# Gated-recurrence heads: seven levels in the first half of a head, the next head's gates, logarithms and scans and this head's output in the second

## The chip, the core and the metric

The kernel runs on one core of a Trainium2 chip. The core has five engines with a queue each: TensorE (PE, with PEld for its weight loads), VectorE (DVE), ScalarE (ACT), GpSimd (POOL) and SyncE (SP), which issues the DMAs. An engine takes its instructions in the order in which they are written, and waits for another one by a semaphore that this other one raises. The metric is the device time of one execution in microseconds, the median of several runs.

## What is computed

The program is a whole two-layer block: a first mixer, a second mixer and an expert layer, on 512 grid tokens and 256 context tokens of width 1024. The change lies in one stage of the second mixer, the gated-recurrence heads. There are eight heads of 128 channels. What a head computes, from the reference:

```python
def hgrn2_forget(f_raw, lb):
    f = lb + (1 - lb) * jax.nn.sigmoid(f_raw.astype(jnp.float32))
    return jnp.log(f), 1 - f
...
    def step(s, inp):
        qc, kc, vc, gc = inp
        gcum = jnp.cumsum(gc, axis=2)
        decay = jnp.exp(jnp.where(causal[:, :, None],
                                  gcum[:, :, :, None, :] - gcum[:, :, None, :, :], -jnp.inf))
        att = jnp.einsum('bhtd,bhtsd,bhsd->bhts', qc, decay, kc)
        glast = gcum[:, :, -1:, :]
        o = (jnp.einsum('bhts,bhsv->bhtv', att, vc)
             + jnp.einsum('bhtd,bhdv->bhtv', qc * jnp.exp(gcum), s))
        s = (jnp.exp(glast[:, :, 0, :, None]) * s
             + jnp.einsum('bhsd,bhsv->bhdv', kc * jnp.exp(glast - gcum), vc))
        return s, o
...
    o = rms_norm(o_f + _flip(o_b), lw['hg_norm_w']).astype(u.dtype)
    o = o * jax.nn.silu(og.reshape(b, t, HG_HEADS, HG_DV))
```

It runs forward and backward over the tokens; both start from a state made by the context tokens. Queries are `silu(q)`. The five inputs of a head (forward forget gate, backward forget gate, query, value, output gate) are products of the normed tokens with five slices of `w_in_2`.

## The kernel before

All of it is in `gated_heads`. Tokens lie in columns, channels in partitions; the 768 tokens are six chunks of 128, two of the context and four of the grid.

**The projection.** A head has five tiles of weights, in the order FF and FB (the two forget gates), Q, V, G (the output gate). SyncE loads each (512 KB) into one of two buffers. ScalarE rounds it (`high`), VectorE subtracts the rounded part from it (`low`), and TensorE multiplies in three products of rounded and remaining parts (`product3`, L243 to L245). The results are cut into eight lots of a head: FF, FB and V have two of 384 columns, Q and G one of 512. A lot is eight units, each of three matmuls; a head thus has 64 units. TensorE does them between the steps of the head before: `fill(count)` takes the next `count` units. Lots alternate between two banks of PSUM, and ScalarE copies a finished lot out (`evict`), which frees its bank.

**A head.** The forget gates go through a sigmoid (`forget`), an affine map (`affine`), a logarithm (`logs`) and a scan that restarts at each chunk (`scan`, into `hg_cum`), forward and backward. `decays` makes the exponentials for the states, `weighted` multiplies them with keys (`hg_kd`) and queries (`hg_qe`). The attention within a chunk of 128 is cut into the diagonal and seven levels of blocks of 1, 2, 4 up to 64 tokens. For a level GpSimd takes two differences of the scans (`diff`, into one of two buffers `hg_dec`), ScalarE takes their exponential in place, VectorE multiplies it with keys and queries (`mixed`, into one of two buffers `hg_mix`), TensorE makes the products (`products`), and VectorE puts them where the level's mask is set (`kept`). `products(0)` is the diagonal, from queries and the sum of keys.

Beside that, TensorE turns the values and, once per direction, the weighted keys into rows; ScalarE copies these out (`hg_vt`, `hg_ktok`); TensorE makes the state updates from them, and VectorE folds the updates into states (`states`). The output is one sum of matmuls from `att` and the states, with its squares (`squares`), their sum by a matmul with ones, the root (`rstd`), and the products `pre` and `tail` with the output gate (`opened`). The query's sigmoid is in `forget` too.

**What sets the order.** A head is a loop over `at` = 1 to 14 on TensorE, ScalarE and VectorE, each with its own list of what stands at which step. A level stands at every second step, 1, 3, up to 13. On ScalarE, step 10 switches the table of functions to the sigmoid and back, and step 12 to the logarithm and back; level 7's exponential is at step 13. The output of a head comes after its step 14, its squares, root and tail at steps 1 to 3 of the next head. GpSimd has only the differences in its queue; it starts a head's when its two scans are done.

## Time and profile before

| | |
|---|---|
| median of 3 runs | 4962.45 us (4962.09 to 4962.82) |
| the profiled execution | 4965.7 us, its span 4963.9 us |
| span of this stage, first weight load to last product | 1449 to 2013 us |
| TensorE busy, whole span | 4008.9 us (81%) |
| VectorE busy | 2604.1 us (52%) |
| ScalarE busy | 1629.9 us (33%) |
| GpSimd busy | 957.4 us (19%) |

Times in the views count from the start of the span. "Busy" of TensorE is counted from modelled ends of pipelined matmuls, so rows of a matmul overlap the next one's start; how long one holds the engine is read from start to start. In a timeline row, `[3.13 <-DVE hg_mix L2685]` says that the engine was idle for 3.13 us before it, and that VectorE's instruction of line 2685 ended that. PEclk is the clock granted to TensorE, 1.00 being 2.4 GHz and 0.50 being 1.2 GHz. About a ninth of the program's time lies in this stage; stages before and after it are the same in both kernels.

### The profile page before, as it was taken

What the parts mean: (1) busy time and instruction counts of PE and PEld (TensorE: products, weight loads), DVE (VectorE), ACT (ScalarE), POOL (GpSimd) and SP (SyncE); (2) the same over time, 40 slices, a digit from 0 to 9 for tenths busy, and PEclk for the clock granted to TensorE, in tenths of its full rate; (3) what the DMA queues carried; (4) which work ended last, traced back from release to release, by engine and by line L of the source; (5) the groups of instructions that cost most, each with busy time, mean ns of one, the idle gap of its engine ahead of it and who ended that gap; (6) DMA issues with size and microseconds to landing.
All of it is one profiled execution on the core that took longest, in us unless ns stands there. A gap on an engine that the chain in (4) does not pass through costs nothing. (4 is left out here: it accounts for less than half of the span.)

```text
span 4963.9 us, 53777 instructions
## 1 busy us (share of the span) xinstructions
PE 4008.9 (81%) x20047; PEld 3308.9 (67%) x20047; DVE 2604.1 (52%) x4384; ACT 1629.9 (33%) x2422; POOL 957.4 (19%) x540
## 2 busy tenths in 40 slices
PE   6445599795948887588887798399897999999996
PEld 5344589662937776577776454287776878888884
DVE  0263678401046666367777201399995545555555
ACT  0332334211034444245455200332563222222222
POOL 0122300120003333011111110043223422222221
PEclk9677899997568998799999899699998999999998
DMA  3100010122411110111110221133456533333332
GB/s 134 45 1 26 22 36 30 34 73 102 157 34 39 43 39 22 40 35 47 43 43 30 115 85 47 51 113 100 136 189 234 196 132 123 127 127 106 122 117 69
DMA packets 134940, 404.74 MB, mean 82 GB/s; under 512 B 16352, under 2 KB 54992, under 8 KB 125008
## 3 DMA queue, kind: packets, MB, share of 16 engines
q1 hardware_dynamic: 134736, 402.01, 23.9%
q8 instruction: 130, 2.13, 0.2%
q14 instruction: 74, 0.61, 0.0%
HBM read 349.51 MB, written 52.45 MB: 81 GB/s over the span
## 5 line engine op out<-in xcount | busy, mean ns | idle before, releaser
L2237 POOL TENSOR_TENSOR ex_vl<-ex_v,ex_vh 128x1024 fp32r<-128x1024 f32 x80 | 192.1, 2401 | 685.6 <-ACT ex_vh L2225 685.6
L243 PE MATMUL ps<-ex_xh,ex_ul 128*128 128x512 f32 x640 | 250.1, 391 | 9.9 <-DVE ex_ul L2244 9.9
L243 PE MATMUL ps<-hT_high,ma_wl 128*128 128x384 f32 (+1 forms) x576 | 233.7, 406 | 25.2 <-DVE ma_wl L3156 25.2
L244 PE MATMUL ps<-ex_xl,ex_uh 128*128 128x512 f32 x640 | 249.7, 390 | 0.0
L245 PE MATMUL ps<-ex_xh,ex_uh 128*128 128x512 f32 x640 | 249.7, 390 | 0.0
L243 PE MATMUL ps<-ex_vh,ex_al 128*128 128x512 f32 x640 | 249.0, 389 | 0.0
L244 PE MATMUL ps<-ex_vl,ex_ah 128*128 128x512 f32 x640 | 249.0, 389 | 0.0
L245 PE MATMUL ps<-ex_vh,ex_ah 128*128 128x512 f32 x640 | 249.0, 389 | 0.0
L2221 ACT ACTIVATE ex_ab<-ps 128x512 f32<-128x512 f32 x80 | 47.8, 598 | 611.2 <-PE ps L245 611.2
L2263 DVE TENSOR_TENSOR ex_acc<-ex_acc,ps 128x512 f32<-128x512 f32 x160 | 109.7, 687 | 248.0 <-PE ps L245 248.0
L1465 DVE TENSOR_TENSOR mg_sg<-mg_sg,ps 128x512 f32<-128x512 f32 x32 | 22.0, 687 | 404.8 <-PE ps L1435 404.2
L2258 DVE TENSOR_TENSOR ex_al<-ex_af,ex_ah 128x512 fp32r<-128x512 f32 x80 | 198.1, 2477 | 61.1 <-ACT ex_ah L2227 61.1
L2400 POOL TENSOR_TENSOR hg_dec<-hg_cum 128x512 f32<-128x512 f32 x56 | 82.3, 1470 | 728.6 <-DVE hg_cum L2664 577.5
L150 PE MATMUL ps<-cond,mod_w 128*128 128x2 f32 x768 | 164.1, 352 | 69.7 <-DMA mod_w<-in_w_ada_cols 42.8
L2852 POOL TENSOR_TENSOR ma_ce<-ma_ce,ma_c 128x512 f32<-128x512 f32 x64 | 94.1, 1470 | 639.6 <-ACT ma_ce L3055 639.6
L243 PE MATMUL ps<-hT_high,hg_wl 128*128 128x384 f32 (+1 forms) x512 | 194.0, 379 | 22.6 <-DVE hg_wl L2640 22.6
L150 PEld LDWEIGHTS ps<-cond,mod_w 128*128 128x128 f32 x768 | 164.0, 333 | 70.5 <-issue 70.5
L245 PE MATMUL ps<-hT_high,ma_wh 128*128 128x384 f32 (+1 forms) x576 | 207.1, 360 | 0.0
L244 PE MATMUL ps<-hT_low,ma_wh 128*128 128x384 f32 (+1 forms) x576 | 206.9, 359 | 0.0
L244 PE MATMUL ps<-hT_low,hg_wh 128*128 128x384 f32 (+1 forms) x512 | 186.7, 365 | 0.0
L245 PE MATMUL ps<-hT_high,hg_wh 128*128 128x384 f32 (+1 forms) x512 | 185.8, 363 | 0.0
L1969 DVE TENSOR_SCALAR sg_two<-iota,chosenT 128x128 f32<-128x128 f32 x512 | 183.6, 418 | 0.0
(510 smaller groups left out, 11064.3 us busy)
## 6 DMA issues: line engine op xcount, KB each, us to landing
ex_u<-in_peer_u SPq DMA_DIRECT2D x80, 512.0 KB, 4.3
ex_v<-in_peer_v SPq DMA_DIRECT2D x80, 512.0 KB, 4.3
gates_by_expert<-sg_gbuf SPq DMA_DIRECT2D x8, 4096.0 KB, 15.1
ma_w<-in_w_in_ma SPq DMA_DIRECT2D x48, 512.0 KB, 3.6
ev_v<-in_peer_v SPq DMA_DIRECT2D x48, 512.0 KB, 3.5
hg_w<-in_w_in_hg SPq DMA_DIRECT2D x40, 512.0 KB, 3.5
ex_g<-gates_by_expert SPq DMA_DIRECT2D x20, 1024.0 KB, 4.8
mg_wg<-in_w_merge SPq DMA_DIRECT2D x16, 1024.0 KB, 5.0
```

The costliest lines, as they stand in the source:

```text
L150: mm = pe.matmul(ps[:, n % 2, 2 * a:2 * a + 2], wt[:, a, k, :], conds[:, k, :], start=(k == 0), stop=(k == KD - 1))
L243: pe.matmul(out, a[1], b[0], start=start, stop=False)
L244: pe.matmul(out, a[0], b[1], start=False, stop=False)
L245: return pe.matmul(out, a[0], b[0], start=False, stop=stop)
L1465: link(dve.tensor_tensor(sg[:, n % 2, a, :], sg[:, n % 2, a, :], ps[:, b + 2 + a, :], ALU.mult))
L1969: ins = dve.tensor_scalar(two[:, t0 + a, :], iota, chosenT[:, 1, t:t + 1], chosenT[:, 2, t:t + 1], ALU.is_equal, ALU.mult)
L2221: act.activation(ab[:, j % 2, :], ps[:, j % 2, :], ACT.Gelu).then_inc(h_read, 1)
L2237: pool.tensor_tensor(vl[:, j], v[:, j % 2], vh[:, j].bitcast(F32), ALU.subtract).then_inc(vl_ready, 1)
L2258: dve.tensor_tensor(al[:, j], af[:, j % 2], ah[:, j].bitcast(F32), ALU.subtract).then_inc(al_ready, 1)
L2263: dve.tensor_tensor(acc[:, n // 2, n % 2, :], acc[:, n // 2, n % 2, :], ps[:, 2 + n % VB, :], ALU.add).then_inc(v_read, 1)
L2400: pool.tensor_tensor(ke, crossed(cums[:, h % 2], size, False, True), crossed(cums[:, h % 2], size, False, False), ALU.subtract)
L2852: pool.tensor_tensor(ce[:, i % 2], ce[:, i % 2], cT[:, P * c:P * c + P].unsqueeze(1).to_broadcast([P, J, P]), ALU.mult).then_inc(ce_scaled, 1)
```

## The change

All seven levels move to steps 1 to 7 of a head, one per step. The second half has the next head's sigmoids (8, 9), affine maps, logarithms and scans (9 to 11), and this head's output (10), squares (11), sum (12), root and tail (13, 14). The query's sigmoid becomes a step of its own (`asked`), and both `decays` and `weighted(h + 1, 0)` of the next head are done by its start. The turning of the values goes behind level 1's products. A table `FILL` gives the units of the projection for each step, 64 in all, as before; evictions are placed where these units end. One of the four table loads per head falls away: behind the sigmoids the logarithm's table comes at once. The instructions on TensorE are the same ones.

```diff
-        LOW_AT = (1, 3, 6, 10, 13)
+        FILL = (4, 5, 5, 5, 5, 5, 5, 5, 5, 4, 5, 4, 4, 3)
...
                     products(0)
                     for at in range(1, 2 * LV + 1):
...
+                        if at <= LV:
+                            products(at)
+                        if at == 1:
+                            pe.wait_ge(evicted, lot_of(h, V, 1) + 1)
                             for c in range(NC):
-                                mm = pe.transpose(turn(c), kds[:, dr, P * c:P * c + P], k.ident[:])
+                                mm = pe.transpose(turn(c), v[:, P * c:P * c + P], k.ident[:])
                                 if c in (3, NC - 1):
-                                    mm.then_inc(kt_done, 1)
-                        if at % 2 == 1:
-                            products((at + 1) // 2)
-                        fill(5 if at <= 8 else 4 if at <= 10 else 2 if at % 2 else 1)
-                        if at in (2, LV + 2):
-                            pe.wait_ge(kt_copied, 2 * u + 2)
-                            if u > 0:
-                                pe.wait_ge(S_ready, u)
-                            for c in ORDER[dr][:-1]:
-                                mm = pe.matmul(U(c), ktok[:, c, :], vt[:, c, :], start=True, stop=True)
-                            mm.then_inc(u_done, 1)
-                    fill(2)
-                    pe.wait_ge(att_kept, (h + 1) * (LV + 1))
-                    pe.wait_ge(S_ready, 2 * h + 2)
-                    for c in range(NXC):
-                        o = ps[:, 5, P * c:P * c + P]
-                        pe.matmul(o, vt[:, C0 + c, :], att[:, c, :], start=True, stop=False)
-                        for dr in range(2):
-                            slot = ORDER[dr][C0:].index(C0 + c)
-                            mm = pe.matmul(o, S[:, dr, slot, :], qe[:, p, dr, P * c:P * c + P], start=False, stop=(dr == 1))
-                    mm.then_inc(o_done, 1)
-                    fill(8)
-                    pe.wait_ge(sq_ready, h + 1)
-                    pe.wait_ge(pre_ready, h + 1)
-                    pe.matmul(ps[:, 5, :], k.ones[:], scr[:], start=True, stop=True).then_inc(ss_done, 1)
+                                    mm.then_inc(vt_done, 1)
+                        if at == 2:
+                            key_rows(0)
+                        if at == 3:
+                            updates(0)
+                        if at == 5:
+                            key_rows(1)
+                        if at == 6:
+                            updates(1)
+                        if at == 10:
+                            pe.wait_ge(att_kept, (h + 1) * (LV + 1))
+                            pe.wait_ge(S_ready, 2 * h + 2)
+                            for c in range(NXC):
+                                o = ps[:, 5, P * c:P * c + P]
+                                pe.matmul(o, vt[:, C0 + c, :], att[:, c, :], start=True, stop=False)
+                                for dr in range(2):
+                                    slot = ORDER[dr][C0:].index(C0 + c)
+                                    mm = pe.matmul(o, S[:, dr, slot, :], qe[:, p, dr, P * c:P * c + P], start=False, stop=(dr == 1))
+                            mm.then_inc(o_done, 1)
+                        if at == 12:
+                            pe.wait_ge(sq_ready, h + 1)
+                            pe.wait_ge(pre_ready, h + 1)
+                            pe.matmul(ps[:, 5, :], k.ones[:], scr[:], start=True, stop=True).then_inc(ss_done, 1)
+                        fill(FILL[at - 1])
...
+                decays(0, 1)
                 for h in range(H):
                     m, n, last = 8 * (h + 1), 5 * (h + 1), h + 1 == H
                     for at in range(1, 2 * LV + 1):
-                        dr = 0 if at <= LV else 1
-                        u = 2 * h + dr
-                        if at % 2 == 1:
-                            i = level_of(h, (at + 1) // 2)
+                        if at <= LV:
+                            i = level_of(h, at)
                             act.wait_ge(diff_ready, i)
                             act.activation(dec[:, (i - 1) % DEC], dec[:, (i - 1) % DEC], ACT.Exp).then_inc(dec_ready, 1)
                         if at == 1:
                             if h > 0:
-                                squares(h - 1)
+                                act.wait_ge(pre_ready, h)
+                            evict(lot_of(h, G))
                             for c0, c1, b in ((0, 4, 2), (4, 6, 3)):
                                 act.wait_ge(vt_done, 2 * h + b - 1)
                                 act.copy(vt[:, c0:c1, :], ps[:, b, 0:P * (c1 - c0)].rearrange("p (c t) -> p c t", c=c1 - c0)).then_inc(vt_copied, 1)
-                        if at in (2, LV + 2):
+                            high(n + FB)
+                        if at == 2 and not last:
+                            evict(m)
+                        if at in (2, 5):
+                            u = 2 * h + (0 if at == 2 else 1)
                             if u > 0:
                                 act.wait_ge(u_done, u)
                             for c0, c1, b in ((0, 4, 2), (4, 6, 3)):
                                 act.wait_ge(kt_done, 2 * u + b - 1)
                                 act.copy(ktok[:, c0:c1, :], ps[:, b, 0:P * (c1 - c0)].rearrange("p (c t) -> p c t", c=c1 - c0)).then_inc(kt_copied, 1)
-                        if at == 2:
-                            if h > 0:
-                                act.wait_ge(pre_ready, h)
-                            evict(lot_of(h, G))
-                            high(n + FB)
-                            if h > 0:
-                                rstd(h - 1)
-                        if not last:
-                            if at == 4:
-                                evict(m)
-                            if at == 5:
-                                evict(m + 1)
-                                high(n + Q)
-                            if at == 7:
-                                evict(m + 2)
-                            if at == 8:
-                                evict(m + 3)
-                                high(n + V)
-                            if at == 10:
-                                evict(m + 4)
-                                high(n + G)
-                        if at == 5:
-                            decays(h, 1)
-                        if at == 10:
+                        if at == 4 and not last:
+                            evict(m + 1)
+                            high(n + Q)
+                        if at == 5 and not last:
+                            evict(m + 2)
+                        if at == 7 and not last:
+                            evict(m + 3)
+                            high(n + V)
+                        if at == 8:
                             act.preload_act_table_set("sigmoid_and_others")
                             if not last:
                                 forget(h + 1)
+                        if at == 9:
+                            if not last:
+                                evict(m + 4)
+                                asked(h + 1)
+                                high(n + G)
                             act.wait_ge(evicted, lot_of(h, G) + 1)
                             opened(h)
-                            act.preload_act_table_set("natural_log_exp_and_others")
-                        if not last and at == 12:
-                            logs(h + 1)
-                    if not last:
-                        evict(m + 5)
-                        decays(h + 1, 0)
-                        evict(m + 6)
-                        high(n + 5 + FF)
-                squares(H - 1)
-                rstd(H - 1)
+                        if at == 10:
+                            if last:
+                                act.preload_act_table_set("natural_log_exp_and_others")
+                            else:
+                                evict(m + 5)
+                                logs(h + 1)
+                        if at == 11:
+                            squares(h)
+                        if at == 12 and not last:
+                            decays(h + 1, 0)
+                            decays(h + 1, 1)
+                            evict(m + 6)
+                        if at == 13:
+                            rstd(h)
+                        if at == 14 and not last:
+                            high(n + 5 + FF)
 
             @block.vector
             def _(dve):
...
+                    n, last = 5 * (h + 1), h + 1 == H
                     for at in range(1, 2 * LV + 1):
-                        if at % 2 == 1:
-                            mixed(h, (at + 1) // 2)
-                        if at in LOW_AT:
-                            low(5 * h + 5 + LOW_AT.index(at))
-                        if at == 1 and h > 0:
-                            pre(h - 1)
-                        if at % 2 == 1:
-                            kept(h, (at - 1) // 2)
-                        if at == 3 and h > 0:
-                            tail(h - 1)
+                        if at <= LV:
+                            mixed(h, at)
+                        if at == 2:
+                            low(n + FB)
+                        if at <= LV + 1:
+                            kept(h, at - 1)
+                        if at == 3:
+                            weighted(h, 1)
                         if at == 4:
                             states(h, 0)
-                        if at == 6:
-                            weighted(h, 1)
-                        if at == 11:
+                        if at == 5:
+                            low(n + Q)
+                        if at == 8:
+                            low(n + V)
                             states(h, 1)
-                        if at == 12 and h + 1 < H:
+                        if at == 9 and not last:
                             affine(h + 1, 0)
                             affine(h + 1, 1)
-                            query(h + 1)
+                        if at == 10:
+                            if not last:
+                                query(h + 1)
+                            opened(h)
+                            low(n + G)
+                        if at == 11 and not last:
+                            scan(h + 1, 0)
+                            scan(h + 1, 1)
                         if at == 12:
-                            opened(h)
-                    if h + 1 < H:
-                        scan(h + 1, 0)
-                    kept(h, LV)
-                    if h + 1 < H:
-                        scan(h + 1, 1)
-                pre(H - 1)
-                tail(H - 1)
+                            pre(h)
+                        if at == 13 and not last:
+                            weighted(h + 1, 0)
+                        if at == 14:
+                            tail(h)
+                            low(n + 5 + FF)
```

What moved, as the instructions stand in the engines' queues in a middle head. Line numbers of the changed kernel differ from those of the kernel before by a few. First ScalarE in the first half; `hg_dec` is a level's exponential, `hg_f<-ps` an eviction, the cast a rounding, `hg_ktok` the turned keys. Before:

```order
L2580 ACTIVATE hg_dec<-hg_dec 128x1024
L2510 COPY hg_f<-ps 128x384
L2580 ACTIVATE hg_dec<-hg_dec 128x1024
L2510 COPY hg_f<-ps 128x384
L2504 CAST hg_wh<-hg_w 128x1024
L2538 ACTIVATE hg_ebl<-hg_cum 128x6
L2540 ACTIVATE hg_qe<-hg_cum 128x512
L2542 ACTIVATE hg_kd<-hg_kd 128x768
L2580 ACTIVATE hg_dec<-hg_dec 128x1024
```

And changed, from level 2 to level 7:

```order
L2592 ACTIVATE hg_dec<-hg_dec 128x1024
L2520 COPY hg_f<-ps 128x384
L2609 COPY hg_ktok<-ps 128x512
L2609 COPY hg_ktok<-ps 128x256
L2592 ACTIVATE hg_dec<-hg_dec 128x1024 x2
L2520 COPY hg_f<-ps 128x384
L2514 CAST hg_wh<-hg_w 128x1024
L2592 ACTIVATE hg_dec<-hg_dec 128x1024
L2609 COPY hg_ktok<-ps 128x512
L2609 COPY hg_ktok<-ps 128x256
L2520 COPY hg_f<-ps 128x384
L2592 ACTIVATE hg_dec<-hg_dec 128x1024 x2
```

The exponentials of three levels (3, 5 and 6) now have an eviction of a lot ahead of them in the same half, with the copies of the keys or a rounding between. The second place is ScalarE from the sigmoids on. Before, `hg_f<-hg_f` of L2516 being the sigmoids and of L2531 the logarithms:

```order
L2617 ACT_TABLE_LOAD
L2516 ACTIVATE hg_f<-hg_f 128x768 x2
L2520 ACTIVATE hg_sg<-hg_q 128x512
L2525 ACTIVATE hg_sg<-hg_gate 128x512
L2622 ACT_TABLE_LOAD
L2580 ACTIVATE hg_dec<-hg_dec 128x1024
L2528 ACT_TABLE_LOAD
L2531 ACTIVATE hg_f<-hg_f 128x768 x2
L2532 ACT_TABLE_LOAD
L2580 ACTIVATE hg_dec<-hg_dec 128x1024
L2510 COPY hg_v<-ps 128x384
```

And changed, L2526 being the sigmoids, L2543 the logarithms and L2560 this head's squares:

```order
L2526 ACTIVATE hg_f<-hg_f 128x768 x2
L2520 COPY hg_q<-ps 128x512
L2532 ACTIVATE hg_sg<-hg_q 128x512
L2514 CAST hg_wh<-hg_w 128x1024
L2537 ACTIVATE hg_sg<-hg_gate 128x512
L2520 COPY hg_v<-ps 128x384
L2540 ACT_TABLE_LOAD
L2543 ACTIVATE hg_f<-hg_f 128x768 x2
L2544 ACT_TABLE_LOAD
L2560 ACTIVATE hg_scr<-ps 128x512
```

The exponentials of levels 6 and 7 have gone from between the table loads, and the first V lot's eviction now stands ahead of the logarithms.

## Rows read from the trace of the kernel before

**Rows 1.** Stretches of one head: window, length, busy us (count) per engine, PEclk, DMA.

```profile
1692.65:1759.30 66.65, 56.02 (x330) 52.30 (x329) 41.99 (x57) 33.05 (x47) 20.76 (x15) 0.92 0.13 40
1759.30:1827.46 68.16, 56.72 (x323) 53.11 (x322) 41.81 (x57) 32.22 (x46) 20.76 (x14) 0.90 0.13 39
```

**Rows 2.** Waits in 1692.65:1759.30: engine, line waited for: total, times, longest.

```profile
DVE hg_mix L2684 <- ACT hg_dec L2580: 20.5, 5, 8.2
```

**Rows 3.** TensorE in order of time: start, length, instruction, count [idle before].

```profile
1692.08 0.38 PE L2485 MATMUL ps<-hg_att,hg_vt 128*128 128x128 f32 x2
...
1694.67 0.47 PE L243 MATMUL ps<-hT_high,hg_wl 128*128 128x512 f32 x1
...
1701.83 1.10 PE L2493 MATMUL ps<-hg_scr,ones 128*128 128x512 f32 x2 [1.31 <-DVE oT L2717]
1702.76 0.82 PE L2437 MATMUL ps<-ident,hg_v 128*128 128x128 f32 x6
1703.41 1.06 PE L2453 MATMUL ps<-hg_q,hg_sg 128*128 128x128 f32 x8
...
1711.20 1.28 PE L2478 MATMUL ps<-hg_vt,hg_ktok 128*128 128x128 f32 x10
1712.31 1.06 PE L2453 MATMUL ps<-hg_mix 128*128 128x128 f32 x8
1713.12 0.42 PE L243 MATMUL ps<-hT_high,hg_wl 128*128 128x384 f32 x1
...
1718.43 1.05 PE L2453 MATMUL ps<-hg_mix 128*128 128x128 f32 x8
...
1742.21 1.75 PE L2453 MATMUL ps<-hg_mix 128*128 128x128 f32 x8 [3.13 <-DVE hg_mix L2685]
...
1752.68 2.04 PE L2453 MATMUL ps<-hg_mix 128*128 128x128 f32 x8 [6.18 <-DVE hg_mix L2685]
```

**Rows 4.** ScalarE in order of time, first half of the same head.

```profile
1705.12 0.86 ACT L2592 COPY hg_ktok<-ps 128x512 f32<-128x512 f32 x2 [0.86 <-PE ps L2467]
...
1716.55 0.48 ACT L2510 COPY hg_f<-ps 128x384 f32<-128x384 f32 x1 [4.75 <-PE ps L245]
1716.92 1.05 ACT L2504 CAST hg_wh<-hg_w 128x1024 fp32r<-128x1024 f32 x1
```

**Rows 5.** The page's DMA issues: tiles, count, KB each, us to landing.

```profile
hg_w<-in_w_in_hg SPq DMA_DIRECT2D x40, 512.0 KB, 3.5
```

**Rows 6.** ScalarE, second half: a logarithm, a table load, an exponential of a level.

```profile
1681.35 0.84 ACT L2531 ACTIVATE hg_f<-hg_f 128x768 f32<-128x768 f32 x1 [0.94 <-DVE hg_f L2647]
1682.21 1.28 ACT L2532 ACT_TABLE_LOAD   x1
1683.51 1.06 ACT L2580 ACTIVATE hg_dec<-hg_dec 128x1024 f32<-128x1024 f32 x1
```

**Rows 7.** VectorE: a scan, the keys' product twice, a mix.

```profile
1690.82 1.75 DVE L2664 TENSOR_TENSOR_SCAN hg_cum<-hg_restart,hg_f 128x768 f32<-128x768 f32 x1
...
1693.48 1.85 DVE L2674 TENSOR_TENSOR hg_kd<-hg_kd,hg_k 128x768 f32<-128x768 f32 x1
...
1719.76 0.94 DVE L2674 TENSOR_TENSOR hg_kd<-hg_kd,hg_k 128x768 f32<-128x768 f32 x1
...
1740.77 0.69 DVE L2684 TENSOR_TENSOR hg_mix<-hg_dec,hg_k 128x512 f32<-128x512 f32 x1 [8.18 <-ACT hg_dec L2580]
```

**Rows 8.** A stretch, TensorE alone: window, length, busy, PEclk, DMA.

```profile
1744.00:1746.00 2.00, 2.00 (x8) 0.51 0.00 0
```

**Rows 9.** TensorE, the next head's sum of squares.

```profile
1768.47 1.10 PE L2493 MATMUL ps<-hg_scr,ones 128*128 128x512 f32 x2 [2.11 <-DVE oT L2717]
```

**Rows 10.** TensorE, level 1 of the first head and the squares ahead of the last.

```profile
1503.27 2.08 PE L2453 MATMUL ps<-hg_mix 128*128 128x128 f32 x8 [0.15 <-DVE hg_mix L2685]
...
1968.85 1.10 PE L2493 MATMUL ps<-hg_scr,ones 128*128 128x512 f32 x2 [1.07 <-DVE oT L2717]
```

**Rows 11.** VectorE, the stage's last product.

```profile
2012.70 0.69 DVE L2723 TENSOR_TENSOR oT<-oT,hg_scr 128x512 f32<-128x512 f32 x1 [2.66 <-ACT hg_scr L2553]
```

36 lines of the change are left out of this document (22 added, 14 removed).

## The prediction

> **What bounds the kernel now.** I read the stretches by head first, then the waits inside one head, then TensorE's order of time, and last ScalarE and VectorE around the two long waits. The stage repeats itself once per head: one head takes 66.65 us from its first GpSimd subtraction to the next one's, and in that time TensorE is busy 56, VectorE 42, ScalarE 33 and GpSimd 21 us [rows 1]. TensorE is the fullest, so the question is what it must do and where it waits.
>
> What it must do in one head, from starts to starts at the full clock [rows 3]: ten units of the next head's projection with 384 columns take 1713.12 to 1718.43, 0.53 us each; eight with 512 columns take 1694.67 to about 1700.35, 0.71 each. A head has 48 and 16 of them: 25.4 + 11.3 = 36.7. The products of a level take 0.81 (1712.31 to 1713.12), eight times: 6.5. Three sets of six transposes at 0.65 (1702.76 to 1703.41): 2.0. Two sets of state updates at 1.11: 2.2. The output 2.6 (1692.08 to 1694.67), the sum of squares 0.93. Together 50.9 us, and the change alters none of it.
>
> Where it waits: three times, 1.3 us for the sum of squares and 3.1 and 6.2 us for the mixes of levels 6 and 7 [rows 3], 10.6 together. In both long ones VectorE in turn waits for ScalarE's exponential, up to 8.2 us [rows 2, 7], which stands behind table loads and sigmoids. The rest, 66.65 - 50.9 - 10.6 = 5.2 us, is what a lower clock takes: behind the 3.1 us wait the granted clock is 0.51, the level of 1.2 GHz [rows 8], and the products behind the 6.2 us wait take 2.04 instead of 1.06 us [rows 3]. Behind the 1.3 us wait they take 1.06, the full clock.
>
> **The change, step by step.** The reordering is meant to take these waits away, and it does: no exponential stands behind a sigmoid any more, and one table load of four goes. But ScalarE's queue is strictly in order, and each level now follows the last at every step. So every exponential of a level stands directly behind an eviction that waits for TensorE. I walk one head, counting the projection's units 1 to 64. From an exponential's start to TensorE's product of that level takes 1.06 + 1.44 us: the exponential's length [rows 6], and the mix of two products from 1740.77 on [rows 7] until TensorE starts at 1742.21 [rows 3]. An eviction starts 0.25 us after its last unit (16 units' end at 1713.12 + 6 x 0.53 = 16.30, the copy at 16.55) and holds ScalarE for 0.38, rounding a weight tile for 0.95, a pair of copies of turned rows for 0.75 (each a tenth less than the row's length, as 1716.55 to 1716.92 shows) [rows 4].
>
> Wait A, ahead of level 2: the transposes of the values now come behind level 1. Transposes to first copy 0.63, copies 0.75, rounding 0.95, exponential 1.06, mix 1.44: 4.83. TensorE has only the transposes and four units, 2.8. It waits 2.0.
> Wait B, ahead of level 3: behind unit 8 come 0.25, the eviction 0.38, the key rows 0.75, 1.06 and 1.44: 3.9. TensorE has one unit left, 0.5. It waits 3.4.
> Wait C, level 5: behind unit 16 come 0.25, 0.38, the rounding 0.95, 1.06, 1.44: 4.1; three units are left, 1.6. It waits 2.5; 0.3 more is for level 4, whose mix stands behind `weighted(h, 1)` on VectorE.
> Wait D, level 6: unit 24 is the last of its step, so nothing is left beside 0.25 + 0.38 + 0.75 + 1.06 + 1.44. It waits 3.9.
> Levels 4 and 7 stand behind no eviction and come in time.
> Wait E, the sum of squares: `logs` is behind the eviction of unit 48. From unit 48: 0.25, the copy 0.48, the table load 1.28, the logarithm 0.84 [rows 6], two scans each with its subtraction 2.66 (1690.82 to 1693.48) [rows 7], `pre` 0.7 and 0.15 to TensorE: 9.0. `pre(h)` is queued behind both scans on VectorE, and the matmul of ones waits for it with eleven units queued behind it. TensorE has units 49 to 53, 2.65. It waits 6.4.
>
> The sum of the waits is 2.0 + 3.4 + 2.8 + 3.9 + 6.4 = 18.5, against 10.6. All five lie one behind the other, since each begins at a unit that TensorE reaches only after the wait before. What the moves of `asked`, `opened`, `query`, `affine`, `states(h, 1)` and the weight tiles' `low` cost, I put at nothing: between units 32 and 44 TensorE has 7.8 us of projection alone, which covers a table load, two sigmoids and the 1.8 us of each `affine`; the V tile is split before unit 41 and the G tile before unit 57. `decays(h + 1, 1)`, moved ahead of the loop, hides under wait E. The weight loads start earlier or when they did; without that cover a late tile would hold TensorE by a load's 3.5 us at most [rows 5].
>
> The clock: the trace has no head with five waits, so I bound its price. With 5.2 us for two waits that were followed by the half clock, one costs at most 2.6. Where the wait for the squares was 2.1 instead of 1.3 us [rows 9], the head took 68.16 instead of 66.65 [rows 1]: 0.8 of the difference is the wait, 0.7 the clock behind it. A wait of 1.3 us cost nothing. I take 1.3 for each of the five, nearer to the 0.7 since A and C are as short as that one: 6.5. A head then takes 50.9 + 18.5 + 6.5 = 75.9 us.
>
> The ends: level 1 of the first head starts at 1503.27 at half clock [rows 10], as now, and all 64 units and the transposes stand behind it; counting 0.8 back to the head's start and 0.8 on for the clock, heads begin at 1503.3. Seven heads project a next one. The last has no units: now it takes from 1967.6 to 2013.4, 45.8 us [rows 10, 11]; its levels then no longer wait for a table, and I put it at 39.5 (between 34 and 46: the first bound is the output at full clock and no wait of VectorE's, the second is today's). End: 1503.3 + 7 x 75.9 + 39.5 = 2074.1, against 2013.4: 60.7 us later. The span before is 4963.9, the execution 4965.7, and the median of the runs 4962.45; on the latter the sum gives **5023 us**.
>
> On the table loads: a load takes 1.28 us, begins 0.02 after the logarithm's end and the exponential 0.02 after its own [rows 6]. The Trainium skill, ScalarE: Activation LUTs (What ACT_TABLE_LOAD costs), adds a drain of 1.38 us to each switch; by it wait E would be 1.4 longer, about 10 us over the stage, and the trace shows no room for it, so the row decides.
>
> **Rivals.** *The clock stays up.* If the waits are too scattered to lower it, a head takes 50.9 + 18.5 = 69.4, the end is at 2028.6, 15 us later: 4978. For it speaks the 1.3 us wait without loss, against it the 2.1 us one. Chance 0.17.
>
> *Faster.* ScalarE is busy only half of a head [rows 1]. If waits A to D are covered, because TensorE reaches each level later than I count and the exponentials are there, only wait E stays: 50.9 + 6.4 + 1.3 = 58.6, an end at 1953, 60 us sooner: 4902. Its place is ScalarE's queue in the first seven steps; it decides once waits and clock together are below (2013.4 - 39.5 - 1503.3) / 7 - 50.9 = 16.3 us per head. Against it: the copy that waits is ahead of the exponential in the queue, whatever the load. 0.06. Half of it, near 16 us, ends within 0.2%: 0.05.
>
> *Slower still.* With the levels packed, VectorE's products fall beside GpSimd's subtractions. The product of the keys took 1.85 us right behind the second scan, when GpSimd's subtractions of the new head begin, and 0.94 later in the head [rows 7]. If each mix on waits A to D becomes 1.2 longer, that is 4.8 per head, 34 us: 5057. The Trainium skill, GPSIMD Engine Reference (Key points), names this contention for VectorE instructions with two SBUF inputs, and by that rule it would be in every mix. Against it: the subtractions of a level are done while VectorE waits, and the mix at 1740.77 took 0.69. 0.07.
>
> That the change does not do what it says I give no chance: the order shows seven exponentials in the first half and none in the second.
>
> **How the numbers follow.** The forecast has 0.65, and by itself lies between 5002 (0.7 us of clock per wait) and 5040 (1.8 per wait). The range reaches from the case with the clock up to a little over that: 4975 to 5045, and leaves out the faster, the equal and the slowest case, 0.18. Of this kernel 0.2%, 10 us, can be told from no change: faster 0.06, the same 0.05, slower 0.89.
>
> **What would show it.** Right: a head of 73 to 78 us; five waits of TensorE per head, four for mixes (2 to 4 us) and one of about 6.4 for the squares; ScalarE's evictions of the gate tiles waiting for TensorE directly ahead of exponentials; a granted clock below 0.9. Wrong: waits for the mixes under 1 us in the first half, or a head under 67 us; then the queue on ScalarE was not what held the levels. If the waits are as said and the head is 69 to 71, only the clock's price was off.

## The result, and the profile after

| | before | changed |
|---|---|---|
| median | 4962.64 us (4962.09 to 4966.86, 4 runs) | 5018.65 us (5016.20 to 5020.86, 4 runs) |
| ratio to before, 95% interval | | 1.0111 (1.0093 to 1.0128) |
| span of the profiled execution | 4963.9 us | 5019.1 us |
| last product of the stage | 2012.70 us | 2069.45 us |
| TensorE busy, whole span | 4008.9 us | 4024.5 us |

The change makes the kernel 56.0 us slower; 60.7 had been forecast. The stage ends 56.7 us later in the trace, so the whole loss lies in this stage. TensorE's own instructions are the same ones and its busy time grew by 15.6 us only, by instructions that ran at a lower clock: the rest is time in which it waits.

Stretches of one head, as in [rows 1]: window, length, busy us (count) for PE, PEld, DVE, ACT and POOL, granted clock, DMA share, GB/s.

```profile
1641.89:1716.14 74.25, 57.53 (x320) 52.77 (x320) 41.08 (x57) 30.84 (x45) 19.46 (x15) 0.91 0.12 36
1789.12:1865.99 76.87, 60.14 (x320) 55.39 (x320) 41.16 (x57) 30.83 (x45) 19.45 (x14) 0.88 0.11 35
1865.99:1939.14 73.15, 56.41 (x320) 51.70 (x320) 41.10 (x57) 30.85 (x45) 19.48 (x15) 0.92 0.12 37
```

A head took 66.65 and 68.16 us before. VectorE and ScalarE have no more to do than then, and both are busy for about half of the head. The waits of the last of these heads, where [rows 2] had `hg_mix` behind `hg_dec` at 20.5 us in five waits: engine, line waited for: total, times, longest.

```profile
ACT hg_f L2520 <- PE ps L245: 24.2, 4, 9.0
...
DVE hg_mix L2697 <- ACT hg_dec L2592: 15.8, 4, 4.5
...
PE ps L2448 <- DVE hg_mix L2698: 10.4, 4, 3.2
...
PE ps L2502 <- DVE oT L2730: 6.3, 1, 6.3
```

Read from below: TensorE waits once for `oT` and four times for mixes; VectorE waits for the exponentials of those mixes, four times too; and ScalarE waits four times for a forget gate's lot (`hg_f<-ps`), that is, for TensorE. Three of these four copies stand ahead of the exponentials of levels 3, 5 and 6; the fourth comes behind level 7. Level 2's exponential stands behind the copies of the turned values (`hg_vt`), which wait for TensorE too. It is a ring: a copy that waits for TensorE stands ahead of the exponential for which TensorE waits next. TensorE's waits one by one, in order of time (start, length, instruction, count, idle before), to be laid beside the three of [rows 3]:

```profile
1884.93 1.13 PE L2448 MATMUL ps<-hg_mix 128*128 128x128 f32 x8 [1.95 <-DVE hg_mix L2698]
...
1892.52 1.21 PE L2448 MATMUL ps<-hg_mix 128*128 128x128 f32 x8 [3.18 <-DVE hg_mix L2698]
...
1904.82 1.13 PE L2448 MATMUL ps<-hg_mix 128*128 128x128 f32 x8 [2.33 <-DVE hg_mix L2698]
...
1912.16 1.13 PE L2448 MATMUL ps<-hg_mix 128*128 128x128 f32 x8 [2.94 <-DVE hg_mix L2698]
...
1940.86 2.04 PE L2502 MATMUL ps<-hg_scr,ones 128*128 128x512 f32 x2 [6.33 <-DVE oT L2730]
```

These are levels 2, 3, 5 and 6 and the sum of squares: waits A to E of the forecast, with 1.95, 3.18, 2.33, 2.94 and 6.33 us. The copies, the exponentials and their order on ScalarE, around level 2 and then around levels 5, 6 and 7:

```profile
1880.69 0.86 ACT L2599 COPY hg_vt<-ps 128x512 f32<-128x512 f32 x2 [1.58 <-PE ps L2478]
1881.44 1.06 ACT L2514 CAST hg_wh<-hg_w 128x1024 fp32r<-128x1024 f32 x1
1882.39 1.06 ACT L2592 ACTIVATE hg_dec<-hg_dec 128x1024 f32<-128x1024 f32 x1
...
1900.97 0.48 ACT L2520 COPY hg_f<-ps 128x384 f32<-128x384 f32 x1 [8.98 <-PE ps L245]
1901.34 1.06 ACT L2514 CAST hg_wh<-hg_w 128x1024 fp32r<-128x1024 f32 x1
1902.29 1.06 ACT L2592 ACTIVATE hg_dec<-hg_dec 128x1024 f32<-128x1024 f32 x1
...
1906.48 0.86 ACT L2609 COPY hg_ktok<-ps 128x512 f32<-128x512 f32 x2 [3.13 <-PE ps L2458]
...
1909.25 0.48 ACT L2520 COPY hg_f<-ps 128x384 f32<-128x384 f32 x1 [1.91 <-PE ps L245]
1909.63 2.00 ACT L2592 ACTIVATE hg_dec<-hg_dec 128x1024 f32<-128x1024 f32 x2
```

ScalarE sits idle for 8.98 us in front of the eviction of 1900.97; level 5's exponential is next but one in its queue. What it does then, 0.38 + 0.95 + 1.06 us from start to start, ends at 1903.35, and TensorE starts level 5 at 1904.82. At 1909.25 it is the same with level 6: eviction, exponential, mix, product at 1912.16.

### The profile page after: what moved, and what is told of

It is laid out like the page before. It is cut to its first block and busy times, and to the rows that moved or that the text cites. A ratio compares the mean times of both kernels' runs of the same rounds, so it can differ in the third digit from the quotient of the medians.

```text
span 5019.1 us, 53770 instructions
## 1 busy us (share of the span) xinstructions
PE 4024.5 (80%) x20047; PEld 3319.4 (66%) x20047; DVE 2599.0 (52%) x4384; ACT 1619.8 (32%) x2415; POOL 946.1 (19%) x540
```

## Experiments

Every kernel is given as its difference from the changed kernel or from the kernel before. A ratio is always to the kernel before, measured on the same chip in turn with it; the changed kernel's own is 1.0111. The kernel of an experiment is called by the experiment's number.

**1. The exponentials ahead of the waiting copies.** The smallest edit that breaks the ring: at each step ScalarE issues the next level's exponential before the step's evictions, roundings and copies.

```diff
-                        if at <= LV:
-                            i = level_of(h, at)
+                        for lv in ((1, 2) if at == 1 else (at + 1,) if at < LV else ()):
+                            i = level_of(h, lv)
```

> The changed kernel with one edit on ScalarE: the exponential of the next level is issued ahead of the eviction, the rounding and the copies of its step, instead of behind them. Theory (the queue): the four waits of TensorE for the mixes (1.95, 3.18, 2.33 and 2.95 us per head) exist only because each exponential stands behind a copy that waits for TensorE. They go, and with them the lower clock behind them; the wait for the squares of 6.3 us stays. A head takes 50.9 + 6.3 + about 1.5 = 59 us instead of 74.9; over seven heads 112 us less than the changed kernel: 4907 us (4895 to 4925). Rival (the level's own loop): the waits come from the chain of GpSimd's subtraction, exponential and mix with two buffers, beside VectorE's other work; then the waits only move, and the time stays within 10 us of 5019.

Measured: 4907.83 us (4904.18 to 4911.65), ratio 0.9883 (0.9866 to 0.9899), as the theory had it. One stretch of a head and its waits, views as above:

```profile
1670.74:1731.04 60.30, 53.97 (x320) 50.32 (x320) 42.20 (x57) 30.97 (x45) 18.59 (x15) 0.92 0.14 44
```

```profile
PE ps L2502 <- DVE oT L2730: 6.3, 1, 6.3
...
DVE hg_mix L2697 <- ACT hg_dec L2592: 1.8, 1, 1.8
```

TensorE's wait for the mixes, 10.4 us a head, is not in the list any more. VectorE's wait for exponentials fell from 15.8 to 1.8 us. The wait for the squares, which this edit does not touch, kept its 6.3 us. So waits A to D, with the clock behind them, came from the order of ScalarE's queue alone: 2.3% of the time, some 113 us. A head, averaged over the six from the second on, took 60.1 instead of 74.9 us: of the 14.9 less, 10.4 are the waits and 4.5 the shorter busy time of TensorE (53.7 instead of 58.2), that is, the clock. Most of what is left of the 113 us lies in the first and the last head, where the same edit applies.

**2. The logarithms ahead of the first V lot's eviction.**

```diff
-                                evict(m + 5)
                                 logs(h + 1)
+                                evict(m + 5)
```

> The changed kernel with one edit on ScalarE: the logarithms of the next head are issued ahead of the eviction of its first V lot. Theory (the queue): the 6.3 us wait for the squares begins at that eviction. Without it the scans are bounded by the affine maps and end some 4 us sooner, the wait falls to about 2.3 us, and 28 us go over seven heads, up to 38 with the clock: 4981 to 4992. Rival (VectorE is the bound of the second half): its affine maps, scans and products would then be late anyway, the wait stays over 5 us and the time within 10 us of 5019.

Measured: 4978.83 us (4973.93 to 4982.98, 10 runs), ratio 1.0023 (1.0014 to 1.0033), a little faster than expected. A head and its waits:

```profile
1697.18:1768.09 70.91, 58.34 (x320) 54.15 (x320) 41.08 (x57) 30.75 (x45) 19.47 (x14) 0.90 0.12 37
```

```profile
PE ps L2448 <- DVE hg_mix L2698: 10.4, 4, 3.2
...
PE ps L2502 <- DVE oT L2730: 2.2, 1, 2.2
```

The mirror image of the first: the waits for mixes are what they were, the wait for the squares fell by 4.1 us. This head is one of the two longest; the six from the second on took 69.3 us on average, 5.7 less than the changed kernel's 74.9. The other 1.5 us are shorter busy time of TensorE (56.7 instead of 58.2), the clock again.

**3. Both, and `pre` between the scans.** Besides edits 1 and 2, VectorE runs one scan at step 11, then `pre(h)`, and the second scan behind it, so that the sum of squares waits for one scan less.

```diff
                         if at == 11 and not last:
                             scan(h + 1, 0)
-                            scan(h + 1, 1)
                         if at == 12:
                             pre(h)
+                            if not last:
+                                scan(h + 1, 1)
```

> Both edits, and on VectorE the product of the output with the gate between the two scans instead of behind both. Theory (the queue): no wait of TensorE over 1 us is left in a head, the clock stays at full, and a head takes the 50.9 us of TensorE's own work, 51 to 53. Over seven heads 155 to 165 us less than the changed kernel: 4855 to 4870. Rival (the level's own loop or VectorE): a head keeps waits of together over 8 us, the time stays above 4900.

Measured: 4859.72 us (4856.84 to 4860.48), ratio 0.9782 (0.9766 to 0.9798). That is inside the range expected, and faster than the kernel before.

```profile
1656.54:1709.44 52.90, 51.62 (x322) 48.55 (x321) 46.51 (x57) 30.77 (x45) 20.47 (x14) 1.00 0.16 50
```

```profile
1665.64 1.13 PE L2448 MATMUL ps<-hg_mix 128*128 128x128 f32 x8 [1.28 <-DVE hg_mix L2698]
```

TensorE is busy for 51.62 of 52.90 us at the full clock; one wait of 1.28 us is left, for one level's mix, where none over 1 us had been expected. That also tests the 50.9 us of work that the forecast had added up from starts: 52.90 - 1.28 = 51.6, so that term was 0.7 too small.

**4. The same waits, without the lower clock.** Matmuls that nobody uses, put ahead of the five waits. They fill the time in which TensorE waited; when the awaited tile is there, nothing has changed but the clock.

```diff
+        BUSY = {1: 2, 2: 3, 4: 2, 5: 3, 11: 6}
...
+                            for _ in range(BUSY[at]):
+                                pe.matmul(ps[:, bank, :], k.ident[:], k.ones[:].unsqueeze(1).to_broadcast([P, NXC, P]), start=True, stop=True)
```

> The changed kernel with sixteen added matmuls per head into banks that hold nothing needed, placed in TensorE's queue right ahead of its five waits: two, three, two, three and six of 128x512, each about 0.93 us, a little less than each wait. They change nothing that is computed; TensorE works where it stood idle. Theory (the clock): of a head's 74.9 us, 7.3 are neither work nor waits, and they are the lower clock behind the waits. With TensorE busy the clock stays at full, the head takes 50.9 + 16.7 + about 1 = 68.6, and seven heads 44 us less than the changed kernel: 4975 (4965 to 4990). Rival: the 7.3 us are starts and ends of instructions and semaphores, not the clock; then the time stays within 10 us of 5019, or rises by what of the added matmuls sticks out.

Measured: 4981.02 us (4978.56 to 4986.36, 7 runs), ratio 1.0027 (1.0015 to 1.0038).

```profile
1634.54:1703.68 69.14, 66.15 (x354) 54.13 (x352) 41.10 (x57) 30.84 (x45) 19.47 (x15) 1.00 0.13 39
```

A program with more matmuls is 38 us faster. The granted clock is 1.00 over the whole head. The seven heads of the changed kernel took 74.9 us on average (below), so without the lower clock a head is 74.9 - 69.1 = 5.8 us shorter, or 1.16 for each of the five waits. That is the net gain: the added matmuls and what is left of the waits take 69.1 - 51.6 = 17.5 us, 0.8 more than the waits alone.

**5. Is `pre` between the scans of any use?** Edits 1 and 2 without it.

> The run with both edits on ScalarE (exponentials first, logarithms ahead of the eviction), but with the product of the output and the gate behind both scans, as in the changed kernel. Theory (the queue): a wait of 2.2 us for the squares comes back in each head, with some 1 us of clock: a head of 56 instead of 52.9 us, seven heads 22 us more than with all three: 4875 to 4890. Rival: the three edits act on one another and this one is worth nothing (under 4866) or nearly all of what the logarithms gave (over 4895).

Measured: 4871.59 us (4870.51 to 4875.56), ratio 0.9807 (0.9791 to 0.9823), somewhat better than expected. It is 12 us behind kernel 3 by the medians, 0.25% by the ratios, so the third edit is of some use, though less than the 22 us expected; the heads say so too, 53.7 and 55.4 us against 52.9. Its heads alternate between two lengths; the last section returns to that.

**6. The kernel before, with its two late exponentials moved.** Is the regrouping itself of use, or only the right queue order? In the kernel before, level 6's exponential goes ahead of the sigmoids and their table load, level 7's ahead of the logarithms, and level 7's mix ahead of the affine maps.

```diff
-                        if at % 2 == 1:
-                            i = level_of(h, (at + 1) // 2)
+                        if at in (1, 3, 5, 7, 9, 10, 12):
+                            i = level_of(h, {10: 6, 12: 7}.get(at, (at + 1) // 2))
...
-                        if at % 2 == 1:
-                            mixed(h, (at + 1) // 2)
+                        if at in (1, 3, 5, 7, 9, 11, 12):
+                            mixed(h, {11: 6, 12: 7}.get(at, (at + 1) // 2))
```

> The kernel before, with its levels at every second step, but level 6's exponential issued ahead of the sigmoids' table load, level 7's ahead of the logarithms', and level 7's mix ahead of VectorE's affine maps. Theory (the queue): what held the kernel before was the same thing, an exponential queued behind other work on ScalarE, so its waits of 3.1 and 6.2 us go without any regrouping of the levels; a head falls from 66.9 to 54 to 58 us, the time to 4880 to 4905. Rival (the levels have to leave the second half): the chain of sigmoid, affine maps, logarithms and scans comes late instead and takes the place of the waits; a head stays above 62 us, the time above 4935.

Measured: 4922.88 us (4920.02 to 4926.41), ratio 0.9910 (0.9894 to 0.9927): between what the two theories had given. Of both long waits for mixes one is gone and 0.7 us is left of the other, but another stands in TensorE's timeline:

```profile
1675.57 0.80 PE L2485 MATMUL ps<-hg_att,hg_vt 128*128 128x128 f32 x2 [6.68 <-DVE hg_att L2697]
```

The output waits for `kept(h, 7)`, which VectorE has behind the affine maps and the first scan.

**7. The same, with `kept(6)` and `kept(7)` moved ahead too.** `kept(h, 6)` goes ahead of the affine maps and `kept(h, 7)` between the two.

```diff
-                        if at % 2 == 1:
-                            kept(h, (at - 1) // 2)
+                        if at in (1, 3, 5, 7, 9, 11, 12):
+                            kept(h, {12: 6}.get(at, (at - 1) // 2))
...
                         if at == 12 and h + 1 < H:
                             affine(h + 1, 0)
+                        if at == 12:
+                            kept(h, LV)
+                        if at == 12 and h + 1 < H:
                             affine(h + 1, 1)
...
                         scan(h + 1, 0)
-                    kept(h, LV)
-                    if h + 1 < H:
                         scan(h + 1, 1)
```

> The kernel before with levels 6 and 7 issued early, as in the run before this one, and on VectorE also the last two masked copies taken out from behind the scans: level 6's ahead of the affine maps, level 7's between them. The run before this one had lost both waits for mixes and got a new one of 6.7 us, TensorE's output waiting for the masked copy of level 7 that stood behind a scan. Theory (the queue): that wait goes too, only about 1 us of wait for the squares stays, and a head falls from 61.7 to 53 to 56 us: 4862 to 4885. Rival (the levels have to leave the second half): the chain of sigmoid, affine maps, logarithms and scans is then late for the next head's level 1 and takes the wait over; a head stays above 59 us, the time above 4900.

Measured: 4936.43 us (4935.32 to 4938.88), ratio 0.9939 (0.9923 to 0.9956): by the time the rival was right, though the wait that came is not for level 1. In TensorE's timeline the wait for the output is gone, and a longer one has come, for the sum of squares (with 1.3 us for a weight tile that VectorE splits late):

```profile
1690.41 2.04 PE L2493 MATMUL ps<-hg_scr,ones 128*128 128x512 f32 x2 [7.64 <-DVE oT L2717]
```

And on ScalarE ahead of it:

```profile
1684.91 1.06 ACT L2580 ACTIVATE hg_dec<-hg_dec 128x1024 f32<-128x1024 f32 x1 [3.21 <-POOL hg_dec L2401]
1685.88 0.58 ACT L2548 ACTIVATE hg_scr<-ps 128x512 f32<-128x512 f32 x1
```

The squares of this head are queued behind the next head's first exponential, which waits for GpSimd's differences, and these for the scans. But the squares are done at 1686.46, and TensorE starts at 1690.41. In between is VectorE:

```profile
1686.00 1.01 DVE L2684 TENSOR_TENSOR hg_mix<-hg_dec,hg_k 128x512 f32<-128x512 f32 x1 [0.57 <-ACT hg_dec L2580]
1686.91 1.55 DVE L2685 TENSOR_TENSOR hg_mix<-hg_dec,hg_q 128x512 f32<-128x512 f32 x1
1688.39 1.21 DVE L2640 TENSOR_TENSOR hg_wl<-hg_w,hg_wh 128x1024 fp32r<-128x1024 f32 x1
1689.52 0.74 DVE L2717 SCALAR_TENSOR_TENSOR oT<-ps,hg_norm_w,hg_gate 128x512 f32<-128x512 f32 x1
```

`pre`, the last of these rows, stands behind level 1's mixes, which wait for the same exponential, and behind a split of weights. So the wait is made by two queues, ScalarE's and VectorE's, and moving the squares alone would not have ended it. The start of each head hangs on the chain sigmoid, affine, logarithm, scan, difference, exponential, and the old layout queues this head's output behind that chain. Kernels 6 and 7 stop at 4923 and 4936, the regrouped kernel with its queues put right at 4860. That supports the regrouping but does not show that it is needed: the old layout with `squares` and `pre` ahead of the next head's level 1, the obvious next step, was not run.

**8. Key copies behind the eviction at level 6.** Wait D measured 2.94, and I had forecast 3.9. In the changed kernel the copies of `hg_ktok` stand ahead of the eviction of step 5; I had counted them behind it. This kernel puts them there.

```diff
+                        if at == 5 and not last:
+                            evict(m + 2)
                         if at in (2, 5):
...
-                        if at == 5 and not last:
-                            evict(m + 2)
```

> The changed kernel with the copies of the turned keys of step 5 issued behind the eviction of unit 24 instead of ahead of it. The prediction had counted them as standing behind it, and the trace shows a wait of 2.95 instead of the 3.9 us forecast. Theory (the queue): the wait for level 6 grows by the 0.75 us that the copies hold ScalarE, to 3.7; 5 us over seven heads, with the clock 3 to 10: 5022 to 5029. Rival (the wait was over-counted for another reason): the wait stays at 2.95 and the time within 2 us of the changed kernel's.

The changed kernel ran again beside it, on the same chip:

> The changed kernel itself, on the same chip as the run with the keys' copies behind the eviction, to compare the two: 5019 us.

Measured: 5027.75 us (5027.07 to 5031.18) against 5014.70 (5012.12 to 5019.36), ratios 1.0124 (1.0107 to 1.0141) and 1.0097 (1.0080 to 1.0114). Level 6's products in TensorE's timeline:

```profile
1689.97 1.13 PE L2448 MATMUL ps<-hg_mix 128*128 128x128 f32 x8 [3.70 <-DVE hg_mix L2698]
```

The wait grew by 0.76, and the other four kept their size. In seven heads that is 5.3 us; 13 were measured by the medians, beyond the 3 to 10 expected. The two traces tell where most of it lies. From the first head's start to the last one's this kernel took 529.9 us and the changed kernel beside it 519.3, 10.6 more; TensorE's busy time in it, with the same instructions, was 402.2 against 397.0. So 5.3 us are waits, 5.2 the lower clock, and some 2 us of the 13 lie outside these heads and have no row.

**9. The kernel before, without its lower clock.** Three and six unused matmuls ahead of the products of levels 6 and 7, in the kernel before, as in experiment 4.

```diff
+                        if h + 1 < H and at in (10, 12):
...
+                            for _ in range(3 if at == 10 else 6):
+                                pe.matmul(ps[:, 5, :], k.ident[:], k.ones[:].unsqueeze(1).to_broadcast([P, NXC, P]), start=True, stop=True)
```

> The kernel before with nine added matmuls of 0.93 us per head into a bank that holds nothing needed, three ahead of the products of level 6 and six ahead of those of level 7, where TensorE waits 3.1 and 6.2 us. They change nothing that is computed. Theory (the clock): of a head's 66.9 us 5.2 are the clock behind these two waits, up to 2.6 each; with TensorE busy they go: a head of 62 to 63, seven heads 27 to 36 us less: 4930 to 4940. Rival (1.2 per wait, as the changed kernel's sixteen added matmuls gave, the rest being starts and ends): a head of 64.5, 17 us less: 4949.

Measured: 4970.57 us (4968.37 to 4977.11, 10 runs), ratio 1.0011 (1.0001 to 1.0020). Both expectations missed: nothing was gained. One head, and TensorE's waits around it:

```profile
1692.37:1760.60 68.23, 61.55 (x340) 52.61 (x339) 41.99 (x57) 32.12 (x45) 20.76 (x15) 0.97 0.13 39
```

```profile
1675.27 1.13 PE L2453 MATMUL ps<-hg_mix 128*128 128x128 f32 x8 [0.56 <-DVE hg_mix L2690]
...
1685.74 1.13 PE L2453 MATMUL ps<-hg_mix 128*128 128x128 f32 x8 [2.61 <-DVE hg_mix L2690]
...
1701.55 2.01 PE L2498 MATMUL ps<-hg_scr,ones 128*128 128x512 f32 x2 [2.31 <-DVE oT L2722]
```

The clock behind the mixes is up (1.13 where [rows 3] had 1.75 and 2.04), and 0.56 and 2.61 us of waiting were left, so the added matmuls held nobody up. Yet the steps are as long as before. From the products of level 6 to those of level 7 it is 10.47 us here (1675.27 to 1685.74) and 10.47 in [rows 3] (1742.21 to 1752.68); from there to the sum of squares 15.81 here and 15.79 before ([rows 3, 9]). What TensorE won behind one wait it waited at the next.

The kernel before shows the same by itself, in the head ahead of the one that [rows 3] shows:

```profile
1675.57 1.13 PE L2453 MATMUL ps<-hg_mix 128*128 128x128 f32 x8 [3.13 <-DVE hg_mix L2685]
...
1686.03 2.05 PE L2453 MATMUL ps<-hg_mix 128*128 128x128 f32 x8 [7.76 <-DVE hg_mix L2685]
```

Here the products of level 6 ran at the full clock, 1.13 instead of 1.75, and TensorE then waited 7.76 instead of 6.18 us: level 7 again came 10.46 us behind level 6, and both heads took 66.65 us. So between these steps the chain over ScalarE and VectorE set the time, and the half clock on TensorE lay beside it.

The heads of this experiment are even longer, 68.2 us each, than most heads before (66.65). That comes behind the squares: there the clock is half (2.01 instead of 1.10), and level 6 follows after 41.95 us (at 1743.50) instead of 40.38 ([rows 3], 1701.83 to 1742.21):

```profile
1743.50 1.13 PE L2453 MATMUL ps<-hg_mix 128*128 128x128 f32 x8 [0.56 <-DVE hg_mix L2690]
```

In that stretch TensorE has no other wait, and the half clock does cost, about 1.6 us.

## Why the prediction was right

**What bounds the kernel.** "TensorE is the fullest, so the question is what it must do and where it waits": its waits did decide. One sentence of this part was wrong, though: the 5.2 us left over before was named as "what a lower clock takes". 0.7 of it is work that was undercounted (51.6 instead of 50.9 us, experiment 3), and most of the rest was not on the path. Averaged over the six heads from the second on, TensorE was busy for 55.4 us a head before, 3.8 more than at the full clock. Experiment 9 takes away about 2 of these (61.55 us busy, less nine added matmuls at 0.91 each as in experiment 4, is about 53.3), and the head gets no shorter; without that clock TensorE waits instead.

**The five waits.** All are where they had been put, and all but D behind exactly what had been named. From the chains of 0.25 + 0.38 + ... on ScalarE:

| wait | forecast | measured |
|---|---|---|
| A, level 2 | 2.0 | 1.95 |
| B, level 3 | 3.4 | 3.18 |
| C, level 5 (and 0.3 for level 4) | 2.8 | 2.33 |
| D, level 6 | 3.9 | 2.94 |
| E, squares | 6.4 | 6.33 |
| sum | 18.5 | 16.7 |

D is the one step with an error of reading. I had counted 0.75 us for key copies behind the eviction, where the order of ScalarE's queue has them ahead, where they pass while it waits anyway. Without them the chain is 0.25 + 0.38 + 1.06 + 1.44 = 3.1; experiment 8 puts them behind and measures 3.70. In C the 0.3 for level 4 did not come; its mix was in time. The sentence that "every exponential of a level stands directly behind an eviction" is too strong, as the walk itself says of levels 4 and 7; level 2 stands behind copies of turned values.

**The clock.** 1.3 a wait, 6.5 a head had been taken, between 0.7 and 2.6. The six heads from the second to the seventh in one window, read as the stretches above:

```profile
1566.56:2016.14 449.58, 349.19 (x1920) 320.90 (x1920) 246.69 (x337) 185.03 (x265) 116.78 (x85) 0.90 0.11 33
```

TensorE is busy for 58.2 us a head, where the same instructions at the full clock took 51.6 (experiments 3 and 5): the lower clock made them 6.6 us longer, 1.3 a wait. Experiment 4 gave back 5.8 of that, net. The size was right, but both bounds had been misread, so that it came out so near was luck. The upper one was made from a leftover that, by experiment 9, was mostly no price of the clock. The lower one took 0.8 of the difference between the two heads of [rows 1] for a longer wait. But two other heads of the trace before have squares' waits as long, 2.06 and 2.10 us, and took 66.65 and 66.66 us. What made the one head 68.16 us long was the clock alone: from its squares to its level 6 it took 41.91 us instead of 40.38. The price behind a wait was 0 or 1.5 there, never the 0.7 that was read.

**A head.** 75.9 had been forecast. From the first level 1 (1505.10) to the last head's (2029.32) seven heads took 524.2 us, 74.9 each. By the measured terms: 51.6 + 16.7 + 6.6 = 74.9. So the waits were forecast 1.8 too long and the work 0.7 and the clock 0.1 too short, which made the forecast 1.0 too long.

**The ends.** The first level 1 and the stage's last product on VectorE:

```profile
1505.10 2.08 PE L2448 MATMUL ps<-hg_mix 128*128 128x128 f32 x8 [10.12 <-DVE hg_mix L2698]
```

```profile
2069.45 0.69 DVE L2736 TENSOR_TENSOR oT<-oT,hg_scr 128x512 f32<-128x512 f32 x1 [2.66 <-ACT hg_scr L2565]
```

Forecast were 1504.1 for the first and 38.7 us from the last head's level 1 to the end. It started 1.0 later, and the last head took 2070.1 - 2029.3 = 40.8, 2.1 more. With 7.1 less for the heads, that is the difference between 60.7 and 56.7. The last head's levels no longer wait for a table, as forecast, but TensorE still waits for five of their mixes (3.1, 3.0, 0.9, 2.4 and 3.2 us) and 2.6 for the output; the forecast had no terms for these waits, only a figure put between two bounds.

**What was put at nothing.** The moves of `asked`, `opened`, `query`, `affine`, the weight tiles and `decays(h + 1, 1)` indeed cost nothing: TensorE has no wait beside the five, none of them for a weight tile.

**The signs.** A head of 73 to 78 us and the five waits came as described. The granted clock was to be below 0.9; it was 0.88 to 0.92 by heads, 0.90 in the mean, so this sign was just missed.

**The table load.** ScalarE and VectorE from the V lot's eviction to `pre`, the stretch of wait E. ScalarE:

```profile
1931.97 0.48 ACT L2520 COPY hg_v<-ps 128x384 f32<-128x384 f32 x1 [4.13 <-PE ps L245]
1932.47 1.28 ACT L2540 ACT_TABLE_LOAD   x1
1933.76 1.58 ACT L2543 ACTIVATE hg_f<-hg_f 128x768 f32<-128x768 f32 x2
```

VectorE:

```profile
1934.64 1.76 DVE L2675 TENSOR_TENSOR_SCAN hg_cum<-hg_restart,hg_f 128x768 f32<-128x768 f32 x1 [4.07 <-ACT hg_f L2543]
...
1937.31 1.75 DVE L2677 TENSOR_TENSOR_SCAN hg_cum<-hg_restart,hg_f 128x768 f32<-128x768 f32 x1
...
1939.97 0.75 DVE L2730 SCALAR_TENSOR_TENSOR oT<-ps,hg_norm_w,hg_gate 128x512 f32<-128x512 f32 x1
```

The chain reads off here: eviction, load, the first logarithm (of two), two scans with their subtractions, `pre`, and TensorE at 1940.86: 8.9 us from 1931.97, against 8.8 in the forecast (9.0 from unit 48, of which 0.25 are ahead of the eviction). Between the load and its neighbours there are 0.02 and 0.01 us. The Trainium skill, ScalarE: Activation LUTs (What ACT_TABLE_LOAD costs), has 1.38 us of drain at each switch. This trace does not show it; by an estimate with the page's figure wait E would have been 7.7, not 6.33.

**The rivals.** *The clock stays up*, 4978, is the case that experiment 4 made by force, at 4981. Its condition did not hold by itself. That the two numbers lie so close is in part chance, for its head of 69.4 us had 50.9 of work and 18.5 of waits, and the measured one of 69.1 has 51.6 and 17.5. *Faster*, 4902 by a head with wait E alone, is what experiment 1 gave (4907.83), but not by the condition that the rival named, that TensorE reaches each level later: there it was the order of the queue, which the prediction had put against this rival. *Slower still*, from VectorE beside GpSimd, left no mark on waits A to D: the mixes that end them took 0.69 and 0.68 us each (at 1883.49, 1891.08, 1903.38 and 1910.72), and GpSimd starts its next subtraction only behind them. The Trainium skill, GPSIMD Engine Reference (Key points), names contention of GpSimd with VectorE's instructions that have two SBUF inputs. This trace agrees where the two fell together: the product of the keys right behind the scans took 1.19 us at 1940.63, beside a subtraction, against 0.94 in [rows 7] later in a head.

## What to carry to other kernels

In an engine's queue, an instruction that waits for the bottleneck must not stand ahead of one that the bottleneck waits for: here four such pairs, moved by one step, were worth 113 us, and the sizes of the waits could be told beforehand from the queue's order and the lengths of its instructions, so long as each copy was put on the right side of the waiting one. When a stage is rearranged, look for that in every queue before judging the new layout: the arrangement that lost 56 us won 108 with two queues put in order. In the kernel before, the half clock cost time in the stretch that TensorE set and none in the stretch that another chain set; so ask of a lower clock, as of any busy time, what would wait instead, and look for a second head in the same trace that ran at the full clock.

## What the runs showed of the hardware

The price of the lower clock depends on what it lies beside: 1.3 us for each wait in the changed kernel by TensorE's busy time (1.16 given back by experiment 4), where the waits follow one another on TensorE; nothing behind the waits for levels 6 and 7 of the kernel before; and 1.5 to 1.6 us behind its squares, where the half clock followed.

And it is no fixed answer to a wait. In kernel 5 two heads in a row, and the squares' wait near the start of each as it stands in TensorE's timeline:

```profile
1658.84:1712.59 53.75, 51.59 (x320) 48.54 (x320) 42.37 (x57) 30.88 (x45) 19.62 (x14) 1.00 0.17 49
1712.59:1767.97 55.38, 53.22 (x320) 49.62 (x320) 42.37 (x57) 30.87 (x45) 19.61 (x14) 0.97 0.15 49
```

```profile
1660.56 1.10 PE L2502 MATMUL ps<-hg_scr,ones 128*128 128x512 f32 x2 [2.16 <-DVE oT L2730]
```

```profile
1714.31 2.02 PE L2502 MATMUL ps<-hg_scr,ones 128*128 128x512 f32 x2 [2.16 <-DVE oT L2730]
```

The same wait of 2.16 us behind the same instructions is followed by matmuls at the full clock in the first head and at the half clock in the second, which makes the second 1.6 us longer; the next head (53.74 us, squares in 1.10) is like the first again. In the changed kernel, too, heads with equal waits differ (73.15 and 76.87 above). So a single head's row is a poor measure of this price; only an average over several heads is.
